# One weight slot issued ahead of the read-back of the expert outputs

## The reference, cut to what matters

```python
hp = hp + _hier_moe(_rmsnorm(hp, g_ffn[i]), *moe_w)          # the experts
hp = hp + _ple(hp, p_prompt[i], g_ple[i], ple_w_proj[i], ple_w_gate[i])
y_prompt = _rmsnorm(hp, g_final)                             # the same for hs

def _ple(h, p_i, g, w_proj, w_gate):                         # "the gate"
    return jax.nn.sigmoid(_rmsnorm(h, g) @ w_gate) * (p_i @ w_proj)
```

## Time and profile before

| | before |
|---|---|
| median of 3 runs | 1007.46 us (1003.53 to 1009.31) |
| profiled execution, its own time | 1010.3 us |
| its span | 1008.6 us |
| TensorE busy | 945.2 us (94% of the span) |
| VectorE busy | 463.2 us (46%) |
| share of TensorE in the chain that ended last | 77% |
| share of DMA in that chain | 15% |
| bytes moved by DMA | 300.29 MB, mean 298 GB/s |

### The profile page before, as it was taken

The page is one execution under the profiler, slowest core; times in us unless marked ns, Lnnn a source line. Parts: engine busy times, 40 slices in busy tenths (PEclk is TensorE's granted clock), DMA queues, the critical chain, the costliest instruction groups (busy, mean ns, idle before and its releaser), DMA issues.

```text
span 1008.6 us, 14123 instructions
## 1 busy us (share of the span) xinstructions
PE 945.2 (94%) x5453; PEld 604.0 (60%) x5453; DVE 463.2 (46%) x1142; ACT 179.8 (18%) x374; POOL 69.9 (7%) x103
## 2 busy tenths in 40 slices
PE   6989999999979989999999999999999999978697
PEld 5767577555536546744478889999744444322275
DVE  4566324543330335786754887555622222211255
ACT  2123214111101103210121110001311111111123
POOL 2433000000000000000000000000121111110000
PEclk9999999899998999999999999999999999999989
DMA  9977698499999999904463333444799999999911
GB/s 358 372 229 257 272 421 360 194 421 421 419 421 419 421 421 395 423 24 167 167 267 112 122 126 126 168 153 149 290 420 417 418 417 419 419 418 422 349 69 47
DMA packets 57736, 300.29 MB, mean 298 GB/s; under 512 B 10146, under 2 KB 18530, under 8 KB 25666
## 3 DMA queue, kind: packets, MB, share of 16 engines
q1 hardware_dynamic: 47952, 282.23, 70.0%
q0 software_dynamic: 7936, 14.17, 4.1%
q10 hardware_dynamic: 1778, 2.94, 0.8%
HBM read 299.86 MB, written 11.51 MB: 309 GB/s over the span
## 4 chain that ended last, share of the span: by engine, by line
PE 77%; DMA 15%; DVE 5%; issue 1%; ACT 1%; SPq 0%; DVEq 0%; POOLq 0%; ACTq 0%
PE ps L2530 9%; DMA ring_sb<-stream 8%; PE ps L2361 8%; PE ps L2569 8%; PE ps L2484 7%; PE ps L2031 6%; PE ps L2370 4%; PE ps L2112 3%; PE ps L2015 3%; DMA scr_sb<-stream 3%; PE ps L2154 3%; PE ps L2121 3%; DMA hn_sb<-stream 3%; PE ps L1790 2%; PE ps L2146 2%; PE ps L1832 2%
## 5 line engine op out<-in xcount | busy, mean ns | idle before, releaser
L2530 PE MATMUL ps<-hn_sb,ring_sb 128*128 128x288 f32 x384 | 96.2, 406 | 0.0
L2361 PE MATMUL ps<-ring_sb,scr_sb 128*64 128x512 f32 x352 | 79.8, 596 | 10.0 <-DMA ring_sb<-stream 9.3
L2530 PEld LDWEIGHTS ps<-hn_sb,ring_sb 128*128 128x128 f32 x384 | 71.7, 190 | 18.7 <-issue 0.5
L2031 PE MATMUL ps<-scr_sb,ring_sb 128*128 128x288 f32 x256 | 64.6, 408 | 0.0
L1449 DVE SCALAR_TENSOR_TENSOR scr_sb<-ps,scr_sb 128x256 f32<-128x256 f32 x16 | 7.7, 484 | 121.3 <-ACT scr_sb L872 121.3
L2361 PEld LDWEIGHTS ps<-ring_sb,scr_sb 128*64 128x64 f32 x352 | 24.3, 137 | 62.4 <-issue 44.2
L2112 PE MATMUL ps<-scr_sb 128*128 128x128 f32 (+1 forms) x384 | 53.5, 296 | 6.2 <-issue 6.2
L2031 PEld LDWEIGHTS ps<-scr_sb,ring_sb 128*128 128x128 f32 x256 | 49.1, 192 | 13.8
L2112 PEld LDWEIGHTS ps<-scr_sb 128*128 128x128 f32 (+1 forms) x384 | 50.2, 205 | 11.6 <-issue 8.3
L2569 PE MATMUL ps<-scr_sb,ring_sb 128*128 128x144 f32 x384 | 51.0, 286 | 0.0
L2569 PEld LDWEIGHTS ps<-scr_sb,ring_sb 128*128 128x128 f32 x384 | 48.6, 190 | 0.0
(11 more groups left out here) (403 smaller groups left out, 1473.2 us busy)
## 6 DMA issues: line engine op xcount, KB each, us to landing
ring_sb<-stream SPq DMA_DIRECT2D x194, 1024.0 KB, 19.3
scr_sb<-stream SPq DMA_DIRECT2D x46, 1024.0 KB, 22.0
hn_sb<-stream SPq DMA_DIRECT2D x8, 1024.0 KB, 24.6
ring_sb<-row_pages POOLq DMA_DIRECT2D x48, 128.0 KB, 5.4
scr_sb<-key_pages SPq DMA_DIRECT2D x24, 192.0 KB, 9.3
ring_sb<-key_pages SPq DMA_DIRECT2D x24, 192.0 KB, 5.5
ring_sb<-row_pages SPq DMA_DIRECT2D x16, 128.0 KB, 2.3
scr_sb<-y_rows SPq DMA_DIRECT2D x4, 512.0 KB, 6.0
```

Source lines behind the costliest of these rows:

```text
L2031: last = mm(bank(PLE_BANK[m % 4], T), ring(s, (m % 2) * D + k * P, P), HG[L][:, k, :], start=(k == 0), stop=(k == KD - 1))
L2361: last = mm(ps[64 * a:64 * a + 64, 2 + b, :], xT[:, k, 64 * a:64 * a + 64], slot(k // 2)[:, (k % 2) * D + a * 512:(k % 2) * D + a * 512 + ...
L2530: last = mm(bank((i + 1) % 4, T), ring(s, (i % 2) * D + k * P, P), hn_t[:, k, :], start=(k == 0), stop=(k == KD - 1))
```

## The change: what it does

The test in the loop over slots moves from slot 246 to slot 247. SyncE issues slot 246 first, then waits for `y_all`, issues the six reads, and then slots 247 to 249. Within each half of the read-back the order of the three blocks becomes 32 rows, 128 rows, 128 rows. Nothing else is changed: the same DMAs, the same semaphores and the same counts.

```diff
-            if s == S_GATE[1]:
+            if s == S_GATE[1] + 1:
                 sp.wait_ge(sem("y_all"), 1)
                 for half in range(2):
-                    for t, (t0, tn) in enumerate(TOK):
+                    for t in (2, 0, 1):
+                        t0, tn = TOK[t]
                         cols = slice(512 * half, 512 * half + 512)
                         sp.dma_start(y12[0:tn, :, t, cols], y_rows[1].rearrange("(k r) n -> r k n", k=2)[t0:t0 + tn, :, cols]
                                      ).then_inc(sem(f"y12_in{half}"), 16)
```

## The result

| | before | changed |
|---|---|---|
| median | 1007.08 us (7 runs, 1003.53 to 1009.31) | 1012.11 us (7 runs, 1009.57 to 1012.83) |
| ratio, 95% interval | | 1.0050 (1.0037 to 1.0064) |
| profiled execution, its span | 1010.3, 1008.6 us | 1012.23, 1010.6 us |

The changed kernel is slower by 5.0 us, and the interval reaches from 3.7 to 6.4 us. The forecast was +2.0 us, 1009.5 with a range of 1005.5 to 1013.0: the direction and the place are right, the size is too small.

A forecast was written before the change was run, and what follows sets the result against it. The prediction took the landing of the reads' first half, which sets TensorE's start, as the bound. Slot +2.5, block order -0.3, clock -0.2 and others 0 gave +2.0 us on the median 1007.46: 1009.5 us, range 1005.5 to 1013.0.

The forecast's parts named there:

- The bound: End of the kernel: the landing of the reads' first half sets TensorE's start and from there the end.
- Slot 246 in front of the reads: Shared DMA queue: the slot delays the first half's landing by +2.5 us, ends +1.1 and +2.5.
- rival 1: Shared queue: the slot fits unseen into the gap before the reads; 1006.5 to 1007.5 us, say 1007.0; chance 0.22.
- What the earlier slot gives: First gate matmul: slot 246 already lands 3.7 us before its first reader, so landing earlier is worth 0.
- The scatter: Last scatter to `y_rows`, beside the earlier slot: taken as 0, bounds 0 and +3.5 us.
- Rival 3: Last scatter is slowed and `y_all` comes later, up to 3.5 us on top of 2.0: 1013.0 us; chance 0.13.
- The order of the blocks: Read-back with the 32-row block first in each half: -0.3 us taken, ends 0 and -2.6.
- rival 2: First half's landing: small block decides it, 2.6 us gained, slot hidden, clock need not fall; 1000.7 us; chance 0.06.
- The clock: TensorE's combination: clock still falls, returning about 3 us after the gate begins; -0.2 us, ends -1.0 and +1.3.
- The sum: Path to the end: +2.5 - 0.3 - 0.2 + 0 = +2.0 us, with nothing else becoming late.
- Rival 4: SyncE's issues: some wait holds it until `y_all`, so the slot is not early; 1007.5 us; chance 0.03.

The follow-up runs named there:

- e1: Kernel before with slot 246 issued ahead of the reads, blocks in the old order: 1010.44 us, ratio 1.0037 to before.
- e6: Kernel before with slot 246 issued between the two halves of the read-back, blocks in the old order: 1008.86 us, ratio 1.0014 to before.
- e9: Kernel before with five more filling matmuls ahead of the first combination: 1004.97 us, ratio 0.9982 to before.
- e10: Changed kernel with eleven more filling matmuls ahead of the first combination: 1007.00 us, ratio 1.0010 to before.
- e3: Kernel before with only half of slot 246 ahead of the reads, the other half behind them, old block order: 1009.18 us, ratio 1.0015 to before.
- e5: Kernel before with slot 246 ahead of the reads but issued only after the wait for `y_all`, old block order: 1010.67 us, ratio 1.0027 to before.
- e7: Kernel before with three more filling matmuls ahead of the first combination: 1004.51 us, ratio 0.9974 to before.
- e2: Kernel before with only the new block order, 32 rows first, slot 246 still behind the reads: 1008.08 us, ratio 1.0005 to before.
- e8: Changed kernel with seven more filling matmuls ahead of the first combination: 1007.56 us, ratio 1.0012 to before.

## Why the prediction was right in its mechanism and wrong in a size

**The bound.** Right: the first half's landing set TensorE's start, and in the two profiles what follows it took as long as before (58.0 against 57.9 us to the end). That they agree so closely is luck in part, since in e1 to e6 the same stretch took 55.3 to 57.5 us.

**Slot 246 in front of the reads.** This term was mis-sized: +2.5 us taken, with +2.5 as the upper end; at the landing it measured +2.9 (e1), +3.0 (e9 to e10) and +3.7 us (changed kernel, 0.9 of them slot 245's own lag); counted from slot 245's last landing it is 3.0 us. Its side was right: the engine that comes last counts, e3 shows that the idle share of the others hid next to nothing, and so rival 1 falls. The prediction had no row of the single engines; the landing times now show how far they lie apart. What the prediction overlooked: it took the price of a slot from a stream of slots (2.5 us), but with this order the late engine moves the slot while the others already move the reads, and there slot 246's last landing came 2.9 (e1) to 3.5 us (changed kernel) behind that of slot 245. In e5, where the reads were not yet under way when most engines moved the slot, it came 2.5 us behind (946.46 and 948.96). That the reads beside it are what slows the slot fits this and the lower rates at a full share, but no run changed the reads alone. The slot's 8 KB packets do not settle it: at the median they took 0.31 us each in the stream, and from 944 to 946, with reads beside them, 0.38 us in the changed kernel but still 0.31 in e1. So this cause is argued and not shown.

**What the earlier slot gives.** Nothing, as forecast; no gate matmul waited for a DMA in either kernel. With the clock held it could have given up to the 0.42 us that e7 waits.

**The scatter.** Unchanged, 8.5 us against 8.8. Rival 3, the one that would have come near the measured time, falls although its time was close.

**The order of the blocks.** -0.3 us taken; e2 gives +0.05% (-0.06% to +0.16%), so nothing that counts, and rival 2's 2.6 us are not there.

**The clock.** -0.2 taken, and 0.1 us in the profiles. But the reasoning was poor: the clock's return was tied to the first gate matmul, 3 us behind it. In the changed kernel it came so, but that was luck: in e1 the clock was back in the microsecond from 959, while the first gate matmul began at 960.73, as its stretch and TensorE's order show:

```profile
959.00:960.00 1.00, 1.00 (x6) 0.62 (x5) 0.66 (x3) 0.43 (x1) 0.00 (x0) 0.99 0.29 123
```

```profile
960.73 0.65 PE L2031 MATMUL ps<-scr_sb,ring_sb 128*128 128x288 f32 x2
```

**The sum.** The profiles give +3.7 at the landing and +0.1 behind it, 3.8 us; the runs give 5.0 (3.7 to 6.4). Whether there is 1 us more, for instance in how long the clock is low in other executions, stays open. Rival 4 falls: the slot was issued at 917.1. The chance of a loss over 0.5%, 0.13, was too low, for the measured one lies on that bound. The measured 1012.11 us also lie just outside the forecast's own range, which ended at 1012; they are inside the stated range only because its end, 1013.0, came from rival 3, whose price was not paid: that much is luck.

## What to carry to other kernels

Idle DMA engines ahead of a critical read are not free room: the read ends with the engine that is furthest behind, and in the gap that one was not idle. Put nothing in the same queue ahead of a read that the next stage waits for, unless it is needed sooner than the read; here the slot had 3.7 us to spare, and none once the clock was held (e7). The larger gain lay beside the transfer, in the idle TensorE that waits for it: a few filling matmuls kept the clock up and took 2.6 us (three, e7) or 1.8 us (five, e9) off the kernel before. They must last until the wait ends, as e8 shows.

## What the runs showed that was not expected

The low clock's length differed between executions of nearly the same code: at one place it was 10 us (before), 14 (changed) and some 7 (e1, from 952 to 959), and no run here shows what sets it. Holding the clock there lowered the median, but did not always narrow the runs: with three fillings they lie 2.9 us apart (e7), with five 5.9 (e9), as far as the first three of before (5.8).
